# The context tile's expert selection done block by block, the weight ring's slots taken in turn, and norm rows combined ahead

## Chip, cores and metric

The kernel runs on one core of a Trainium2 chip. The metric is the time of one execution on the device in microseconds (us), as the median of several runs.

## What is computed

A transformer-like step of two layers over 128 context tokens and 512 latent tokens (width 1024, float32 throughout). In each layer the tokens pass a modulation, a combined input projection, a gated linear recurrence, grouped-query attention, a mix of the two branches and an output projection, a layer norm, and then a mixture of experts whose choice is the part that matters here:

```python
q = (x @ w_query).reshape(T, PEER_HEADS, 2, PEER_HALF)          # 8 heads, 2 halves of 128
s = jnp.einsum('thpd,hpnd->thpn', q, sub_keys)                  # 128 keys per half
s_top, i_top = lax.top_k(s, PEER_TOPK)                          # 16 of 128, per head and half
cand_s = s_top[:, :, 0, :, None] + s_top[:, :, 1, None, :]      # 16 x 16 sums per head
best_s, best_pos = lax.top_k(cand_s, PEER_TOPK)                 # 16 of 256
expert = jnp.take_along_axis(cand_i, best_pos, axis=-1)
gate = jax.nn.softmax(best_s, axis=-1)
# then, per token: gelu(x . u[expert]) * gate, summed over the rows v[expert]
x  = layer_norm(ALPHA * x + gate1 * (y @ w_out), ln1_g, ln1_b)
h2 = x * (1 + scale2) + shift2                                  # what the experts read
```

## The kernel before

The tokens lie in five tiles of 128: tile 0 is the context, tiles 1 to 4 are latent. All five engines run one instruction stream each, written out by hand, and are tied by semaphores. A loop of two passes runs over the layers.

**The weight ring.** Every dense weight comes in blocks of 2 MB into `ring`, which has two slots. SyncE's queue holds all loads of a layer in a fixed order (`load(s, block)`, L282 to L288): it waits until TensorE has released slot `s` (`w_free[s]`), then issues the transfer; TensorE waits on `w_full[s]`. A load that waits for its slot holds up all loads behind it. The 39 blocks of a layer are first taken in order, slot = block number mod 2; the last four of them (blocks 35 to 38) are the expert query weights, used for the context tile. Then blocks 25 to 38 (eight for the branch mix, two for the output projection, four for the queries) are loaded a second time, for the latent tiles, starting again with slot 0. After the fourth of these last query blocks comes the first block of the next layer, in slot 0.

**The context tile after attention.** TensorE makes the branch mix of the context tile (L1068), then the output projection in two halves (`tokenwise`, L722). VectorE adds the branch to `x` (`add_branch`, L1286 and L1288), takes the statistics of the layer norm (`norm_stats`, L1257 to L1261), gets a square root from ScalarE, and applies the norm in six steps (`norm_apply`, L1269 to L1279): subtract and scale, times gain, plus base (this is the new `x`), times scale2, plus shift2 (this is `h2c`). Only then TensorE turns `h2c` (L746), makes the four blocks of queries (`query_block`, L1096), each covering two heads, and behind each the scores of the block before (`score_block`, L1108). ScalarE copies queries (L615) and scores (L622) out of PSUM; after the fourth block of scores it signals `stage_ready` once. VectorE's `choose(gates[0])` then selects: 16 of 128 for 16 head halves (`first_level`, L1295 to L1306), the sums (`candidates`, L1512 and L1514), 16 of 256 for 8 heads (`second_level`), positions (L1525 to L1531), two look-ups of three steps over 2048 elements (L1537, L1541, L1544), and the expert numbers (L1548). With `stage_free` VectorE lets ScalarE write into `late` again, since `stage` and `work`, in which the selection works, are also the buffers `sg` of the latent mix. `idx_ready` lets GpSimd begin to gather the context tile's expert rows (L346).

**The latent mix.** TensorE goes on with eight blocks for the latent tiles (L1127), 32 matmuls of 512 columns each. Block n uses PSUM banks 0 to 3 when n is even and 4 to 7 when n is odd; the sigmoids of ScalarE (L641, behind `stage_free`) and the products of VectorE (`mix`, L1705, L1707) release them. VectorE puts 16 dot products of the context tile with gathered rows (L1660) behind each `mix`. Then follow the latent output projection (L722), the four norms of the latent tiles, the weighted sum of 96 gathered rows of the context tile on VectorE (`ctx_sum`, L1667) beside the latent queries and scores on TensorE (L1161, L1172), the last 32 of those rows on TensorE (L751, L753), the selection for the first latent tile (`choose(gates[1])`), and then the four latent tiles' experts, which take most of the kernel. The selections for the other latent tiles are cut in pieces between the dot products there (`piece`).

## Time and profile before

| | us |
|---|---|
| median of 3 runs | 6148.5 (6143.8 to 6161.4) |
| the profiled execution's own time | 6114.0 |
| its span, first to last instruction | 6112.2 |
| TensorE matmuls busy | 5046.7 (83%) |
| VectorE busy | 3742.0 (61%) |
| ScalarE busy | 825.7 (14%) |
| GpSimd busy | 1726.2 (28%) |

All times of the trace count from the start of the span. In a row of the timeline stand the start, the duration, the engine (PE is TensorE, DVE VectorE, ACT ScalarE, POOL GpSimd; SPq is SyncE's queue), the line of the kernel, the operation, what it writes and reads, and how many instructions are merged in the row; the number in brackets is how long the engine was idle before, with what ended it. A float32 matmul appears as two records. The first layer's stretch from the context norm to the first latent gathers is 1130 to 1720 us, the second layer's 4172 to 4760 us.

### The profile page before, as it was taken

What the parts mean: (1) busy time and instruction counts of PE and PEld (TensorE: products, weight loads), DVE (VectorE), ACT (ScalarE), POOL (GpSimd) and SP (SyncE); (2) the same over time, 40 slices, a digit from 0 to 9 for tenths busy, and PEclk for the clock granted to TensorE, in tenths of its full rate; (3) what the DMA queues carried; (4) which work ended last, traced back from release to release, by engine and by line L of the source; (5) the groups of instructions that cost most, each with busy time, mean ns of one, the idle gap of its engine ahead of it and who ended that gap; (6) DMA issues with size and microseconds to landing.
All of it is one profiled execution on the core that took longest, in us unless ns stands there. A gap on an engine that the chain in (4) does not pass through costs nothing. (4 is left out here: it accounts for less than half of the span.)

```text
span 6112.2 us, 62289 instructions
## 1 busy us (share of the span) xinstructions
PE 5046.7 (83%) x18696; PEld 2745.5 (45%) x18696; DVE 3742.0 (61%) x7541; ACT 825.7 (14%) x2126; POOL 1726.2 (28%) x1567
## 2 busy tenths in 40 slices
PE   5998789897977777777769987998979777777776
PEld 3787367643432222222237873676434322223222
DVE  0366333378888787876604663323788787878665
ACT  0121033000111001010101210330001110010100
POOL 0000000055644444443300000000657444444432
PEclk8999889998999999999989988899989899999999
DMA  6111100487999999999941111014979999999997
GB/s 230 45 47 46 46 1 27 180 331 296 385 373 400 409 403 411 398 416 421 368 179 45 46 46 46 1 43 177 346 295 379 374 407 409 403 412 396 416 421 328
DMA packets 251837, 1589.74 MB, mean 260 GB/s; under 512 B 28849, under 2 KB 38705, under 8 KB 105649
## 3 DMA queue, kind: packets, MB, share of 16 engines
q0 software_dynamic: 221184, 1342.28, 54.8%
q1 hardware_dynamic: 15936, 224.93, 9.6%
q10 hardware_dynamic: 14448, 19.42, 0.9%
q8 instruction: 112, 1.84, 0.1%
q14 instruction: 157, 1.28, 0.1%
HBM read 1581.27 MB, written 5.24 MB: 260 GB/s over the span
## 5 line engine op out<-in xcount | busy, mean ns | idle before, releaser
L751 PE MATMUL banks<-arena 128*128 128x512 f32 x1152 | 652.0, 649 | 304.4 <-PEq L1208 302.3
L365 POOL DMA_INDIRECT arena<-in_peer_uv,eidx x512 | 563.2, 1100 | 738.7 <-POOLq L364 708.8
L1646 DVE SCALAR_TENSOR_TENSOR arena<-arena 128x1024 f32<-128x1024 f32 x512 | 626.8, 1224 | 146.3 <-DMA arena<-in_peer_uv,eidx 133.7
L346 POOL DMA_INDIRECT arena<-in_peer_uv,eidx x512 | 592.5, 1157 | 335.9 <-POOLq L345 203.3
L753 PE MATMUL banks<-arena 128*128 128x512 f32 x1152 | 615.9, 617 | 0.0
L332 POOL COPY late<-arena 128x640 f32 x16 | 11.4, 719 | 1875.5 <-POOLq L331 1875.5
L417 ACT ACTIVATE late<-late 128x1 f32<-128x1 f32 (+1 forms) x1026 | 208.3, 203 | 2374.3 <-ACTq L416 2374.1
L751 PEld LDWEIGHTS banks<-arena 128*128 128x128 f32 x1152 | 202.0, 201 | 710.2 <-issue 709.8
L751 PE MATMUL banks<-ring,arena 128*128 128x512 f32 x512 | 301.1, 672 | 238.5 <-PEq L1208 238.5
L825 PE MATMUL banks<-hT,ring 128*128 128x320 f32 x1536 | 432.5, 433 | 2.9 <-PEq L822 2.9
L365 POOL DMA_INDIRECT ring<-in_peer_uv,eidx x256 | 286.3, 1118 | 477.3 <-POOLq L364 454.5
L753 PEld LDWEIGHTS banks<-arena 128*128 128x128 f32 x1152 | 230.1, 200 | 297.6 <-issue 297.6
L722 PE MATMUL banks<-ring,hT 128*128 128x512 f32 x800 | 349.1, 598 | 10.5 <-PEq L720 10.5
L1646 DVE SCALAR_TENSOR_TENSOR ring<-ring,arena 128x1024 f32<-128x1024 f32 x256 | 313.0, 1223 | 68.3 <-DMA ring<-in_peer_uv,eidx 67.6
L1646 DVE SCALAR_TENSOR_TENSOR hT<-hT,arena 128x1024 f32<-128x1024 f32 x256 | 313.7, 1225 | 61.4 <-DMA hT<-in_peer_uv,eidx 54.2
L365 POOL DMA_INDIRECT hT<-in_peer_uv,eidx x256 | 267.7, 1046 | 281.8 <-POOLq L364 264.0
L751 PE MATMUL banks<-hT,arena 128*128 128x512 f32 x512 | 284.6, 638 | 62.5 <-PEq L1208 60.1
L825 PEld LDWEIGHTS banks<-hT,ring 128*128 128x128 f32 x1536 | 283.9, 190 | 108.0 <-issue 4.5
L1660 DVE SCALAR_TENSOR_TENSOR arena<-arena,late 128x1024 f32<-128x1024 f32 x256 | 304.7, 1224 | 41.4 <-DMA arena<-in_peer_uv,eidx 33.6
L1638 DVE TENSOR_SCALAR arena<-ident,late,arena 128x128 f32<-128x128 f32 x512 | 210.3, 411 | 186.5 <-ACT late L417 169.8
L1638 DVE TENSOR_SCALAR arena<-ident,late 128x128 f32<-128x128 f32 x512 | 196.9, 385 | 178.7 <-ACT late L417 165.2
L753 PE MATMUL banks<-ring,arena 128*128 128x512 f32 x512 | 290.0, 651 | 0.0
(255 smaller groups left out, 7312.1 us busy)
## 6 DMA issues: line engine op xcount, KB each, us to landing
ring<-in_wblk SPq DMA_DIRECT2D x106, 2048.0 KB, 7.9
arena<-in_peer_uv,eidx POOLq DMA_INDIRECT x1024, 9.0
arena<-in_lnrows ACTq DMA_DIRECT2D x6, 1024.0 KB, 8.2
arena<-in_sk ACTq DMA_DIRECT2D x4, 1024.0 KB, 9.0
hT<-in_peer_uv,eidx POOLq DMA_INDIRECT x256, 11.9
ring<-in_peer_uv,eidx POOLq DMA_INDIRECT x256, 12.3
x<-in_x_sample ACTq DMA_DIRECT2D x1, 2048.0 KB, 18.3
late<-in_state ACTq DMA_DIRECT2D x32, 64.0 KB, 1.8
```

What stands on the lines that cost most here:

```text
L332: nc.gpsimd.tensor_copy(qstage[b], qkv[:, :, bass.ds((2 * i + b) * P, P)]).then_inc(qst_ready[b], 1)
L346: nc.gpsimd.indirect_dma_start(grow[j], None, ins["peer_uv"], bass.IndirectOffsetOnAxis(ap=eidx[:, n, r:r + 1].bitcast(U32), axis=0)).then ...
L365: nc.gpsimd.indirect_dma_start(gslot[j], None, ins["peer_uv"].rearrange("(e h) d -> e (h d)", h=2), bass.IndirectOffsetOnAxis(ap=eidx[:, n ...
L417: nc.scalar.activation(av[:, first:last], av[:, first:last], ACT.Gelu).then_inc(gelu_ready, 1)
L722: last = nc.tensor.matmul(banks[:, b, :], lhs[:, k, t * P:(t + 1) * P], ring[:, s, k, :], start=k == 0, stop=k == KD - 1)
L751: nc.tensor.matmul(banks[:, 4, :], diag[n], row[:, 0:CB], start=start, stop=stop, skip_group_check=True).then_inc(diag_used, 1)
L753: nc.tensor.matmul(banks[:, 5, :], diag[n], row[:, CB:D], start=start, stop=stop, skip_group_check=True).then_inc(free, 1)
L825: last = nc.tensor.matmul(banks[:, bank + f, 0:HALF], ring[:, b, k, c * P:(c + 1) * P], hT[:, k, tok], start=k == 0, stop=k == KD - 1)
L1638: V.tensor_scalar(diag[r % DIAGS], ident[:], av[:, r:r + 1], gate_of[:, r:r + 1], ALU.mult, ALU.mult).then_inc(diag_ready, 1)
L1646: V.scalar_tensor_tensor(u, u, 1.0, h2[:, t - 1, :], ALU.mult, ALU.mult, accum_out=av[:, r:r + 1])
L1660: V.scalar_tensor_tensor(grow[j], grow[j], 1.0, h2c, ALU.mult, ALU.mult, accum_out=av[:, r:r + 1]).then_inc(row_free[j], 1)
```

## The change

Three edits.

1. **Selection in blocks.** ScalarE signals `stage_ready` after each of the four score blocks. VectorE runs first level, sums, second level, positions and both look-ups for the two heads of a block as soon as its scores are there, four times; only the expert numbers are made once at the end. A new helper `look_up_both` does both look-ups of a block at once, one in `stage` and one in `work`. The exponential of the gates is still done once, after the last block.
2. **Ring slots in turn.** The second run of blocks 25 to 38 starts with slot 1 instead of slot 0, and TensorE's uses of them are swapped to match. The fourth latent query block so lies in slot 0, the third in slot 1.
3. **Norm rows combined ahead.** Before the context tile's branch is added, VectorE makes `scale = gain * (1 + scale2)` and `shift = shift2 + base * (1 + scale2)`. The statistics of each half are taken right behind that half's `add_branch`. After the first step of the norm, `h2c` is made straight from it in two steps and signalled; the new `x` is made after that.

```diff
@@ sync queue
                 load(0, l * NB + NB - 1)
-                with sp.Fori(0, (B_PQ - B_MIX) // 2) as i:
+                with sp.Fori(0, (NB - B_MIX) // 2) as i:
                     for s in range(2):
-                        load(s, l * NB + 2 * i + B_MIX + s)
-                with sp.Fori(0, (NB - B_PQ) // 2) as i:
-                    for s in range(2):
-                        load(s, l * NB + 2 * i + B_PQ + s)
+                        load(1 - s, l * NB + 2 * i + B_MIX + s)
@@ ScalarE, score_block
                     nc.scalar.copy(stage[:, n * CB:(n + 1) * CB], banks[:, b, :]).then_inc(bank_free[b], 1)
+                    act.drain().then_inc(stage_ready, 1)
...
                 score_block(3)
-                act.drain().then_inc(stage_ready, 1)
                 exponentiate(gates[0])
@@ TensorE
                 for n in range(KD):
-                    s, f = n % 2, n % 2
+                    s, f = (NB + n) % 2, n % 2
...
-                        tokenwise(2 * t - 2 + h, h, yT, t - 1).then_inc(to_dve[2 * t - 2 + h], 1)
+                        tokenwise(2 * t - 2 + h, 1 - h, yT, t - 1).then_inc(to_dve[2 * t - 2 + h], 1)
...
                 with pe.Fori(0, 2) as i:
-                    for s in range(2):
+                    for n in range(2):
+                        s = 1 - n
                         pe.wait_ge(w_full[s], 16)
...
@@ VectorE
+                def look_up_both(h):
+                    c, one = slice(h * TOPK, (h + 2) * TOPK), slice(h * TOPK * TOPK, (h + 2) * TOPK * TOPK)
+                    spots = [y[:, one] for y in (stage, work)]
+                    keys = tif[:, 2 * h:2 * h + 4].rearrange("p (h a) k -> p h a k", a=2)
+                    for a in range(2):
+                        V.tensor_tensor(r3(spots[a], TOPK), (paf, pbf)[a][:, c].unsqueeze(2).to_broadcast([P, 2 * TOPK, TOPK]),
+                                        iota[:].unsqueeze(1).to_broadcast([P, 2 * TOPK, TOPK]), ALU.is_equal)
+                    dve.drain()
+                    for a in range(2):
+                        spot = spots[a].rearrange("p (h s k) -> p h s k", h=2, s=TOPK)
+                        V.tensor_tensor(spot, spot, keys[:, :, a, :].unsqueeze(2).to_broadcast([P, 2, TOPK, TOPK]), ALU.mult)
+                    dve.drain()
+                    for a in range(2):
+                        V.tensor_reduce((e1, e2)[a][:, c], r3(spots[a], TOPK), AX.X, ALU.add)
                     dve.drain()
...
+                dve.wait_ge(ln_full, 16)
+                dve.sem_inc(ln_full, -16)
+                gain, base, scale, shift = ln1_ctx[:, 0], ln1_ctx[:, 1], bc_ctx[:, 1], bc_ctx[:, 2]
+                V.tensor_tensor(rows_ctx, base, scale, ALU.mult)
+                dve.drain()
+                V.tensor_tensor(shift, shift, rows_ctx, ALU.add)
+                V.tensor_tensor(scale, scale, gain, ALU.mult)
+                xc, stats, mv = x[:, 0, :], small[:, 64:76], small[:, 128:130]
                 for h in range(2):
                     add_branch(0, h, 4 + h, bc_ctx, tmp_ctx)
-                dve.wait_ge(ln_full, 16)
-                dve.sem_inc(ln_full, -16)
-                norm_stats(0)
-                norm_apply(0, ln1_ctx, bc_ctx, h2c)
-                choose(gates[0])
+                    V.bn_stats(stats[:, 6 * h:6 * h + 6], xc[:, h * CB:(h + 1) * CB])
+                dve.drain()
+                V.bn_aggr(mv, r3(stats, 6))
+                dve.drain()
+                V.tensor_scalar(small[:, 0:1], mv[:, 1:2], EPS, None, ALU.add)
+                inverse_root(1)
+                V.tensor_scalar(xc, xc, mv[:, 0:1], small[:, 0:1], ALU.subtract, ALU.mult)
+                dve.drain()
+                V.tensor_tensor(h2c, xc, scale, ALU.mult)
+                dve.drain()
+                V.tensor_tensor(h2c, h2c, shift, ALU.add).then_inc(h2_ready, 1)
+                V.tensor_tensor(xc, xc, gain, ALU.mult)
+                dve.drain()
+                V.tensor_tensor(xc, xc, base, ALU.add)
+                for n in range(4):
+                    dve.wait_ge(stage_ready, 1)
+                    dve.sem_inc(stage_ready, -1)
+                    first_level(stage, 4 * n, 4 * n + 4)
+                    candidates(2 * n, 2 * n + 2)
+                    second_level(2 * n, 2 * n + 2)
+                    positions(gates[0], 2 * n, 2 * n + 2)
+                    look_up_both(2 * n)
+                expert_ids()
```

`candidates` and `positions` get a range of heads; without it they do all eight, as before.

## Rows read from the trace of the kernel before

**Rows 1.** The page: its first line.
```profile
span 6112.2 us, 62289 instructions
```

**Rows 2.** Timeline of TensorE, first layer, queries and scores to latent mix.
```profile
1149.35 1.94 PE L746 MATMUL banks<-ident,late 128*128 128x128 f32 x8 [11.94 <-PEq L744]
1152.71 8.86 PE L1096 MATMUL banks<-hT,ring 128*128 128x128 f32 x64 [1.43 <-PEq L1093]
...
1171.11 7.38 PE L1096 MATMUL banks<-hT,ring 128*128 128x128 f32 x64 [0.20 <-PEq L1093]
...
1196.10 16.00 PE L1127 MATMUL banks<-hT,ring 128*128 128x512 f32 x32 [6.48 <-PEq L1125]
...
1254.35 13.97 PE L1127 MATMUL banks<-hT,ring 128*128 128x512 f32 x32 [0.41 <-PEq L1125]
```

**Rows 3.** The same timeline in the second layer.
```profile
4194.79 10.10 PE L1096 MATMUL banks<-hT,ring 128*128 128x128 f32 x64 [1.43 <-PEq L1093]
...
4239.18 16.80 PE L1127 MATMUL banks<-hT,ring 128*128 128x512 f32 x32 [5.77 <-PEq L1125]
```

**Rows 4.** Timeline of SyncE's queue and time to landing, window 1170 to 1200.
```profile
1187.55 0.93 SPq L286 DMA_DIRECT2D ring<-in_wblk  x2
...
DMA to landing us min/median/max: 8.3/10.4/12.5
```

**Rows 5.** Windows: span, then busy time by engine, PEclk, DMA share, GB/s.
```profile
1190.00:1196.00 6.00, 0.00 (x0) 0.00 (x0) 5.42 (x34) 0.32 (x1) 0.00 (x0) 0.78 1.00 425
1196.00:1200.00 4.00, 3.90 (x5) 1.85 (x6) 4.00 (x31) 0.00 (x0) 0.00 (x0) 0.50 0.78 332
```

**Rows 6.** Timeline of VectorE, first layer, the context norm.
```profile
1130.05 0.69 DVE L1286 TENSOR_TENSOR arena<-banks,arena 128x512 f32<-128x512 f32 x1 [9.45 <-DVEq L1285]
...
1139.22 1.29 DVE L1257 BATCH_NORM_STATS2 small<-x 128x6 f32<-128x512 f32 x2 [0.18 <-DVEq L1686]
...
1143.92 1.22 DVE L1273 TENSOR_TENSOR x<-x,arena 128x1024 f32<-128x1024 f32 x1
```

**Rows 7.** Timeline of ScalarE: first score copy and first latent sigmoids.
```profile
1171.03 0.58 ACT L622 COPY late<-banks 128x512 f32<-128x512 f32 x1 [0.95 <-ACTq L621]
...
1246.79 1.09 ACT L641 ACTIVATE late<-banks 128x512 f32<-128x512 f32 x2
```

**Rows 8.** Timeline of VectorE, first layer, the context selection.
```profile
1227.84 0.29 DVE L1525 TENSOR_TENSOR late<-late 128x128 f32<-128x128 f32 x1
...
1228.91 2.29 DVE L1537 TENSOR_TENSOR late<-late,iota 128x2048 f32<-128x2048 f32 x1
...
1243.10 0.29 DVE L1548 SCALAR_TENSOR_TENSOR late<-late 128x128 f32<-128x128 f32 x1
...
1249.54 0.69 DVE L1707 TENSOR_TENSOR arena<-late 128x512 f32<-128x512 f32 x1
```

**Rows 9.** Timeline of VectorE: the selection's first instruction and its wait.
```profile
1190.50 2.61 DVE L1295 MAX8 late<-late 128x8 f32<-128x128 f32 x13 [41.45 <-DVEq L1567]
```

**Rows 10.** Timeline of TensorE and VectorE, first layer, latent output projection and third norm.
```profile
1434.69 57.36 PE L722 MATMUL banks<-ring,arena 128*128 128x512 f32 x128 [6.20 <-PEq L720]
...
1495.42 0.16 DVE L1269 RECIPROCAL small<-small 128x1 f32<-128x1 f32 x1 [4.36 <-DVEq L1268]
```

**Rows 11.** Groups by line, VectorE, windows 1519 to 1664 and 4563 to 4704.
```profile
L1667 DVE SCALAR_TENSOR_TENSOR late<-arena,late 128x1024 f32<-128x1024 f32 x96 | 123.3, 1285 | 20.7 <-DMA arena<-in_peer_uv,eidx 11.2 <-issue 2.4
...
L1667 DVE SCALAR_TENSOR_TENSOR late<-arena,late 128x1024 f32<-128x1024 f32 x96 | 123.3, 1284 | 16.3 <-DMA arena<-in_peer_uv,eidx 6.7 <-issue 2.4
```

**Rows 12.** Timelines of SyncE's queue, VectorE and TensorE in and behind the weighted sum.
```profile
1621.90 0.33 SPq L286 DMA_DIRECT2D ring<-in_wblk  x1
...
1632.21 8.17 DVE L1667 SCALAR_TENSOR_TENSOR late<-arena,late 128x1024 f32<-128x1024 f32 x6 [2.68 <-DMA arena<-in_peer_uv,eidx]
...
1663.45 3.19 DVE L1295 MAX8 late<-late 128x8 f32<-128x128 f32 x16 [0.29 <-DVEq L1567]
...
1652.70 1.15 PE L1172 MATMUL banks<-arena 128*128 x8 [0.31 <-PEq L1170]
```

More of the change, by code:

```diff
@@ L182, in build @@
         tmp_ctx = arena[:, 20480:20992]
+        rows_ctx = arena[:, 20992:22016]
         tmp_lat = arena[:, 5120:5632]
@@ L1183, in _ @@
                             if u:
-                                score_part(8 * i + 4 * s + u - 1, u - 1)
-                        score_part(8 * i + 4 * s + 3, 3)
+                                score_part(8 * i + 4 * n + u - 1, u - 1)
+                        score_part(8 * i + 4 * n + 3, 3)
                         pe.drain().then_inc(w_free[s], 1)
@@ L1509, in first_level, with candidates @@
                           work[:, a * NKEYS:b * NKEYS], NKEYS, b - a)
-                def candidates():
-                    V.tensor_copy(tif, ti.bitcast(U32))
-                    halves_v = tv.rearrange("p (h a) k -> p h a k", a=2)
-                    V.tensor_tensor(stage.rearrange("p (h a b) -> p h a b", h=PEER_H, a=TOPK),
-                                    halves_v[:, :, 0, :].unsqueeze(3).to_broadcast([P, PEER_H, TOPK, TOPK]),
-                                    halves_v[:, :, 1, :].unsqueeze(2).to_broadcast([P, PEER_H, TOPK, TOPK]), ALU.add)
+                def candidates(a=0, b=PEER_H):
+                    out = slice(a * TOPK * TOPK, b * TOPK * TOPK)
+                    V.tensor_copy(tif[:, 2 * a:2 * b], ti[:, 2 * a:2 * b].bitcast(U32))
+                    halves_v = tv[:, 2 * a:2 * b].rearrange("p (h a) k -> p h a k", a=2)
+                    V.tensor_tensor(stage[:, out].rearrange("p (h a b) -> p h a b", h=b - a, a=TOPK),
+                                    halves_v[:, :, 0, :].unsqueeze(3).to_broadcast([P, b - a, TOPK, TOPK]),
+                                    halves_v[:, :, 1, :].unsqueeze(2).to_broadcast([P, b - a, TOPK, TOPK]), ALU.add)
                     dve.drain()
@@ L1522, in second_level, with positions @@
                           work[:, a * n:b * n], n, b - a)
-                def positions(gate_of):
-                    V.tensor_tensor(r3(gate_of, TOPK), r3(bs, TOPK), r3(bs, TOPK)[:, :, 0:1]
-                                    .to_broadcast([P, PEER_H, TOPK]), ALU.subtract).then_inc(soft_ready, 1)
-                    V.tensor_scalar(bq.bitcast(U32), bp.bitcast(U32), 4, None, ALU.logical_shift_right)
-                    V.tensor_scalar(bp.bitcast(U32), bp.bitcast(U32), 15, None, ALU.bitwise_and)
-                    dve.drain()
-                    V.tensor_copy(paf, bq.bitcast(U32))
-                    V.tensor_copy(pbf, bp.bitcast(U32))
+                def positions(gate_of, a=0, b=PEER_H):
+                    c = slice(a * TOPK, b * TOPK)
+                    high, low4 = bq[:, c], bp[:, c]
+                    op = V.tensor_tensor(r3(gate_of[:, c], TOPK), r3(bs[:, c], TOPK), r3(bs[:, c], TOPK)[:, :, 0:1]
+                                         .to_broadcast([P, b - a, TOPK]), ALU.subtract)
+                    if b == PEER_H:
+                        op.then_inc(soft_ready, 1)
+                    V.tensor_scalar(high.bitcast(U32), low4.bitcast(U32), 4, None, ALU.logical_shift_right)
+                    V.tensor_scalar(low4.bitcast(U32), low4.bitcast(U32), 15, None, ALU.bitwise_and)
+                    dve.drain()
+                    V.tensor_copy(paf[:, c], high.bitcast(U32))
+                    V.tensor_copy(pbf[:, c], low4.bitcast(U32))
+                    dve.drain()
@@ L1682, in _ @@
                 dve.sem_inc(bc_ready, -1)
+                dve.wait_ge(ln_full, 16)
[6 more added lines that the diff above has]
+                xc, stats, mv = x[:, 0, :], small[:, 64:76], small[:, 128:130]
                 for h in range(2):
                     add_branch(0, h, 4 + h, bc_ctx, tmp_ctx)
-                dve.wait_ge(ln_full, 16)
-                dve.sem_inc(ln_full, -16)
-                norm_stats(0)
-                norm_apply(0, ln1_ctx, bc_ctx, h2c)
-                choose(gates[0])
+                    V.bn_stats(stats[:, 6 * h:6 * h + 6], xc[:, h * CB:(h + 1) * CB])
[10 more added lines that the diff above has]
+                V.tensor_tensor(xc, xc, gain, ALU.mult)
+                dve.drain()
+                V.tensor_tensor(xc, xc, base, ALU.add)
[8 more added lines that the diff above has]
+                expert_ids()
                 V.tensor_scalar(e1, e1, layer_base[:], 2.0, ALU.add, ALU.mult)
```

## The prediction

> **What bounds the kernel now.** I read the page first [rows 1]: the span is 6112.2 us, the profiled execution's own time 6114.0, so 1.8 us lie around the span. The median of the runs shown is 6148.5, 34 us more than the profiled one; nothing in the trace tells why, so I work out a difference inside the profiled span and subtract it from the median. The change touches a stretch of some 100 us in each layer, so shares of the whole say nothing. I followed the chain of each layer from the context norm to the first latent gathers in the timelines.
>
> In the stretch TensorE is the engine that sets the pace, with two holes. It idles 11.94 us before it turns `h2c` [rows 2], because VectorE's norm chain runs meanwhile [rows 6]. And it idles 6.48 us (5.77 in the second layer) before the latent mix [rows 2, 3]. What ends the second hole is a weight load: SyncE issues two loads together at 1187.55 [rows 4], right after the last query block of the context has left slot 0 (L1096; four blocks, the last ends about 1187.2), and the first lands 8.3 us later, at 1195.9; the mix starts at 1196.10. The second of the two loads went into slot 1, free some 8.7 us earlier; it had only stood behind the first in the queue. In that hole the DMA share is 1.00 and TensorE's granted clock falls: 0.78 over the hole, 0.50 over the next 4 us, its lower level of 1.2 GHz [rows 5]. So the first half block of the mix takes 16.00 and 16.80 us where the later ones take 13.97 [rows 2, 3].
>
> VectorE's selection starts at 1190.50 after 41.45 us without work [rows 9] and ends its last look-up at 1243.10 [rows 8]. It looks like the bottleneck, but is not: what waits for it is PSUM bank 0, which ScalarE's first sigmoid behind `stage_free` releases at 1246.79 + 0.6 = 1247.4 [rows 7], and TensorE wants it for the third mix block at 1254.35 and gets it with an idle time of only 0.41 us [rows 2]. There are 7.0 us of slack.
>
> **Part 1, norm rows ahead.** Added before the norm: three instructions over 1024 elements, 1.22 us each and 0.08 between them [rows 6], 3.9 us together. VectorE idles 9.45 us just there [rows 6], waiting for the output projection, so they cost nothing; without that cover they would cost 3.9. The gain rows they read were loaded at the start of the stage, long before. Removed from the chain to `h2_ready`: one half of the statistics (half of 1.29), now taken in the idle time before the second half arrives, about 0.65; two full-width steps, 2 x 1.30 = 2.6; the wait before the statistics that shows 0.18 [rows 6], of which I count 0.05. Sum 3.3 us per layer. The two steps for the new `x` come behind, 2.6 us, while VectorE has nothing to do until the first scores. Everything on TensorE after it moves 3.3 us earlier. The hole is then 8.6 us. The clock also fell within a hole of 6.5 us [rows 5], so it will be low again: the first query block takes 8.86 or 10.10 us against 7.38 [rows 2, 3], a price of 1.5 to 2.7 us that I leave as it is; its bounds are a gain of 1.2 and a loss of 1.2 per layer.
>
> **Part 2, ring slots in turn.** The first mix load no longer needs slot 0 but slot 1, left by the third query block, which ends at 1171.11 + 7.38 = 1178.5 [rows 2]. Issue at 1178.8, landing 8.3 later [rows 4], 1187.1. TensorE finishes the last scores at 1196.10 - 6.48 = 1189.6. So the load is there 2.5 us before it is wanted, and all of this shifts together by part 1. The hole goes down to the 0.41 us that stands between blocks: 6.07 us in the first layer, 5.36 in the second. With no hole the clock does not fall, and the slow start goes as well: 16.00 - 13.97 = 2.03 and 16.80 - 13.97 = 2.83. Sum 8.1 and 8.2 us. Which wait is late next? The third mix block. It moves from 1254.35 to 1254.35 - 3.3 - 8.1 = 1242.95, and the bank it needs would come at 1247.4 - 3.3 = 1244.1 with the old selection, a stall of 1.1 us. That is all that part 3 is worth on the path. The later blocks of the mix take 28 us each and need one load each, so they are unaffected. In the wait before the latent output projection, 6.20 us [rows 10], a load follows the last mix block in both orders: nothing changes there. The two issues that follow in SyncE's queue after the first mix load go at the same releases as before, or earlier.
>
> The Trainium skill ("TensorE: Matmul & The Clock Gate", The HAM clock gate) says that where the clock changes depends on when the chip happens to look, so that the same kernel has a different number of slow matmuls from run to run. The two layers here agree (2.03 and 2.83). By that page the 4.9 us that I count for the clock in the two layers could be anything between 4 and 6 in a given run.
>
> One more effect lies 450 us later. In the weighted sum the VectorE waits for gathered rows because weight loads share the DMA engines. In the first layer these waits sum to 11.2 us and in the second to 6.7 [rows 11]. The first layer has one load more: the next layer's first block, issued at 1621.90 when the third latent query block has left slot 0; 7.6 us later VectorE falls dry for 2.68 us [rows 12]. In the changed order slot 0 holds the fourth query block, whose last scores end at 1652.70 + 1.15 = 1653.9 [rows 12], so that load is issued at 1654.1 - 11.4 = 1642.7. The weighted sum ends at about 1663.2 [rows 12] - 11.4, and without the stall at 1647.4, that is 4.7 us after the issue and before the 7.6 us have passed. So 11.2 - 6.7 = 4.5 us go, once. Bounds: 0, if the load now delays the 32 rows that TensorE sums after it, and 4.5. TensorE takes 1.72 us for a row and has eight of them gathered ahead, 13.8 us, against one load of 8 to 12 us [rows 4]. I take 4.4.
>
> **Part 3, selection in blocks.** Work: before, 1243.10 - 1190.50 = 52.6 us [rows 8, 9]. Look-ups were 14.2 (1228.91 to 1243.10) as six instructions of 2.29; now per block six of 512 elements, in pairs, 0.69 each [rows 8] with 0.08 behind each pair's end, about 4.15, times four 16.6. Three more calls each of first and second level, 0.5 us each for waiting out their five steps (an estimate from gaps of 0.1 us between steps), 3.0. Sums and positions in four small sets instead of one, about 3.7 more. Together 61.8 us. Lower bound 52.6 (nothing added); upper bound 67, if each of the 39 added small instructions cost 0.29, as 128 elements do [rows 8], and the calls 3.0. It starts when the first score block is copied, 1171.03 + 0.58 [rows 7] - 3.3 = 1168.3. Blocks of scores come every 8.7 us, a block of selection takes 15.4, so VectorE never waits again and ends at 1230.1, with bounds 1221 and 1235. From the last look-up to bank 0 it took 4.3 us, so the bank is free at 1234.4, 8.5 us before the 1242.95 at which it is wanted. The drain and the signal that ScalarE adds behind each score copy hold up only its next query copy, which it waits 7 us for anyway. GpSimd starts its gathers 13 us earlier, but VectorE's first dot products still stand behind the second mix block, so this gains nothing.
>
> The Trainium skill ("VectorE: DVE Perf Modes", The TRN2 errata) speaks against this part: every VectorE instruction has a fixed cost whatever its size. This trace agrees, 0.69 us for 512 elements where a quarter of 2.29 is 0.57 [rows 8]; by the page's 58 cycles the 18 added look-up instructions would cost 1.1 us (an estimate), half of my 2.4.
>
> **Does it reach the end?** The latent output projection follows the mix directly (57.36 us [rows 10]); the square root of the third latent norm waits for TensorE's turn behind it, 4.36 us [rows 10], so VectorE hangs on TensorE there, and from then on the fourth norm, the weighted sum and the second selection on VectorE. All of it moves with the mix. The gathers of the latent tiles start behind that selection.
>
> Sum: first layer 3.3 + 8.1 + 4.4 = 15.8; second layer 3.3 + 8.2 = 11.5; together 27.3 us. The profiled execution would take 6086.7, the median 6148.5 - 27.3 = **6121.2 us**.
>
> **Rivals.**
> - *The load only moves its stall.* The next layer's first block delays the rows that TensorE adds, and the 4.4 come back: gain 22.9, 6125.6. For it: TensorE's sum of 32 rows gates the fourth latent gather. Chance 0.15.
> - *The hole stays.* The mix load, though issued earlier, lands late, because it collides with the load of the fourth query block, or the slot is released later than I read. Then only part 1 and the 4.4 are left, 6.6 + 4.4 = 11 us: 6137.5. Against it: two loads together took 8.3 and 12.5 us [rows 4], and they are issued over 8 us apart now. Chance 0.1.
> - *The expert stages swallow it.* They fill the rest of both layers and hang on gathers; a shift may change how transfers meet, and the gain is within 18 us: about 6138. Chance 0.1.
> - *Slower: the selection becomes the bound.* VectorE's small instructions cost much more than their rows, and the third mix block waits for `stage_free`. It begins to show at 61.8 + 8.5 = 70.3 us of selection, and the layer is slower than before from 70.3 + 11.4 = 82, that is 20.4 us a block. At 25 us a block the selection takes 100 and each layer loses 18: 6148.5 + 36 - 4.4 = 6180. Against it: no row has an instruction at such a price. Chance 0.04.
>
> **How the numbers follow.** The forecast has 0.61. Its own uncertainties (clock 2.4, runs of the same kernel that differ by up to 18 us around the median) give 6110 to 6132. The range takes in the first three rivals: 6108 to 6139. About 0.3%, 18.4 us, is what a measurement can tell from no change. Faster by more than that: nearly all of the forecast and of the first rival, 0.75. Within: the second and third and what run-to-run spread takes, 0.21. Slower: 0.04.
>
> **What the profile will show.** TensorE's idle time before the first L1127 is near 0.4 us and its first row 13.97; the granted clock stays at 1.00 there. Idle before L746 is about 8.6. VectorE's first MAX8 comes 22 us earlier, and its last look-up 13 us. No wait for the bank in the third mix block. The load for the next layer falls behind the weighted sum, whose DMA waits drop to about 7. The prediction is wrong if TensorE still waits before the mix, if the selection takes over 70 us, or if the stretch is 11 us shorter and the span is not.

## The result, and the profile after

| | median us | range | runs |
|---|---|---|---|
| before, same measurement | 6153.0 | 6143.8 to 6162.6 | 6 |
| after | 6122.7 | 6117.3 to 6133.6 | 6 |

The ratio is 0.995 with a 95% interval of 0.9936 to 0.9964: 30.4 us less, with an interval of 22 to 39 us, clear of no change. The forecast was 27.3 us less. The profiled execution of the changed kernel took 6133.6 us, 11 us over its median, whereas that of before was 34 us under the median of its own runs. So the two traces must not be subtracted as wholes: the spans are 6112.2 and 6131.8, as if the kernel had become slower. What follows compares stretches.

The page of the changed kernel, its first line and the line of busy times; VectorE has 84 instructions and 21 us more than before:

```profile
span 6131.8 us, 62461 instructions
...
PE 5046.9 (82%) x18696; PEld 2744.1 (45%) x18696; DVE 3763.4 (61%) x7625; ACT 825.4 (13%) x2126; POOL 1722.6 (28%) x1567
```

Timeline of TensorE, changed kernel, first layer, from the turn of `h2c` (L744, before L746) over the last scores (L1106) and the latent mix (L1125) to the latent output projection (L720). The last line is from a later window of the same view:

```profile
1148.24 1.94 PE L744 MATMUL banks<-ident,late 128*128 128x128 f32 x8 [8.63 <-PEq L742]
...
1186.25 2.02 PE L1106 MATMUL banks<-arena 128*128 128x128 f32 x16 [0.41 <-PEq L1104]
1188.11 13.90 PE L1125 MATMUL banks<-hT,ring 128*128 128x512 f32 x32
...
1244.27 13.97 PE L1125 MATMUL banks<-hT,ring 128*128 128x512 f32 x32 [0.41 <-issue]
...
1427.00 57.07 PE L720 MATMUL banks<-ring,arena 128*128 128x512 f32 x128 [8.56 <-PEq L1136]
```

Against [rows 2]: the idle time before the turn is 8.63 instead of 11.94, there is no idle time at all before the mix where 6.48 stood, the first half block takes 13.90 instead of 16.00, and the third mix block begins without a wait (0.41). Of the four, the first three are the gain. The last line has 8.56 against 6.20 in [rows 10], for a wait that I had put at no change; more traces below say whether that is a loss.

The same view in the second layer:

```profile
4200.23 1.94 PE L744 MATMUL banks<-ident,late 128*128 128x128 f32 x8 [8.63 <-PEq L742]
...
4241.74 13.90 PE L1125 MATMUL banks<-hT,ring 128*128 128x512 f32 x32
...
4478.61 57.03 PE L720 MATMUL banks<-ring,arena 128*128 128x512 f32 x128 [6.23 <-PEq L718]
```

Windows of the changed kernel over the end of the scores and the start of the mix (span, then busy time of TensorE's matmuls and weight loads, VectorE, ScalarE, GpSimd, then the granted clock, the DMA share and GB/s). Where the clock was 0.78 and 0.50 and the DMA share 1.00 [rows 5], it is now 1.00 throughout, and the transfers are spread out:

```profile
1184.00:1190.00 6.00, 5.59 (x38) 4.47 (x37) 5.59 (x27) 1.76 (x3) 0.00 (x0) 1.00 0.53 167
1190.00:1200.00 10.00, 10.00 (x24) 4.39 (x24) 8.88 (x37) 0.00 (x0) 0.00 (x0) 1.00 0.29 121
```

Timeline of VectorE, changed kernel, context selection: the first row opens the first block of two heads, the next is one of its three look-up rows, and the two MAX8 rows open the second and the third block; the last row is the step that makes the expert numbers:

```profile
1170.48 0.87 DVE L1294 MAX8 late<-late 128x8 f32<-128x128 f32 x4 [20.10 <-DVEq L1731]
...
1182.04 1.29 DVE L1545 TENSOR_TENSOR late<-late,iota 128x512 f32<-128x512 f32 x2
...
1186.24 0.87 DVE L1294 MAX8 late<-late 128x8 f32<-128x128 f32 x4 [0.18 <-DVEq L1731]
...
1202.20 0.87 DVE L1294 MAX8 late<-late 128x8 f32<-128x128 f32 x4 [0.18 <-DVEq L1731]
...
1233.24 0.29 DVE L1570 SCALAR_TENSOR_TENSOR late<-late 128x128 f32<-128x128 f32 x1
```

A block takes 15.8 and 16.0 us (forecast 15.4), the whole from 1170.48 to 1233.5 63.1 us (forecast 61.8, upper bound 67). ScalarE's first sigmoid of the mix follows, timeline of ScalarE:

```profile
1236.92 1.08 ACT L639 ACTIVATE late<-banks 128x512 f32<-128x512 f32 x2
```

so the bank that the third mix block needs is free at about 1237.5, 6.8 us before 1244.27, where TensorE takes it.

**How much of the gain stands behind the mix?** I measure from the start of the idle time before the turn (start of that row minus its bracket, which is where the context's output projection ends) to the start of the latent output projection.

| | layer 1 | layer 2 | both |
|---|---|---|---|
| before | 1434.69 - 1137.41 = 297.3 | 4479.13 - 4179.48 = 299.7 | |
| after | 1427.00 - 1139.61 = 287.4 | 4478.61 - 4191.60 = 287.0 | |
| less | 9.9 | 12.6 | 22.5 |
| forecast | 11.4 | 11.5 | 22.9 |

**The weighted sum, where the last 4.4 us were to come from.** Groups of VectorE by line, changed kernel, weighted sum in the first layer, against [rows 11]. The waits for gathered rows did fall, from 11.2 to 5.9 us, as forecast (6.7):

```profile
L1689 DVE SCALAR_TENSOR_TENSOR late<-arena,late 128x1024 f32<-128x1024 f32 x96 | 123.3, 1284 | 15.4 <-DMA arena<-in_peer_uv,eidx 5.9 <-issue 2.1
```

But look at what comes behind the sum, timeline of VectorE:

```profile
1647.10 2.66 DVE L1689 SCALAR_TENSOR_TENSOR late<-arena,late 128x1024 f32<-128x1024 f32 x2 [0.26 <-DMA arena<-in_peer_uv,eidx]
1681.01 3.19 DVE L1294 MAX8 late<-late 128x8 f32<-128x128 f32 x16 [31.24 <-DVEq L1589]
```

The latent selection starts 31 us after the sum has ended, where in [rows 12] it followed at once (0.29). What it waits for are the latent scores, which come late because TensorE has holes among the latent queries. Timeline of TensorE, changed kernel, and of ScalarE, which copies those scores:

```profile
1554.11 2.07 PE L1170 MATMUL banks<-arena 128*128 x8 [7.13 <-issue]
1574.45 15.54 PE L1159 MATMUL banks<-hT,ring 128*128 128x512 f32 x32 [18.27 <-issue]
```

```profile
1561.89 0.27 ACT L669 COPY late<-banks 128x128 f32 x1 [8.28 <-ACTq L668]
...
1573.56 0.27 ACT L669 COPY late<-banks 128x128 f32 x1 [11.02 <-ACTq L668]
```

The "issue" in brackets means that the profile shows nothing for which TensorE waited. The ends of matmuls in a row are modelled; ScalarE's copies say when scores really were there. The last group of scores of the first query block, which by the first row ended at 1556.2, was copied at 1573.56, the group before it at 1561.89. TensorE was not waiting for weights: SyncE's queue, below, shows that the slot that TensorE leaves with these scores was free only at 1574.76, and that signal is TensorE's own. Then the windows of the same 10 us, first the changed kernel, then the kernel before:

```profile
1574.76 1.40 SPq L287 DMA_DIRECT2D ring<-in_wblk  x1
```

```profile
1555.00:1565.00 10.00, 1.18 (x6) 0.88 (x5) 9.27 (x8) 0.65 (x2) 7.59 (x8) 0.50 0.97 365
```

```profile
1555.00:1565.00 10.00, 9.25 (x29) 4.66 (x28) 9.27 (x8) 1.98 (x5) 7.84 (x8) 1.00 1.03 396
```

Both kernels gather expert rows at full DMA share there. In the one TensorE is busy for 1.18 us of 10, in the other for 9.25. Either the change made these holes, or the profiled execution of before happened to be without them. That was the first question for the runs.

### The profile page after: what moved, and what is told of

It reads as the page before. It is cut to its first block and busy times, and to the rows that moved or that the text cites. A ratio compares the mean times of both kernels' runs of the same rounds, so it can differ in the third digit from the quotient of the medians.

```text
span 6131.8 us, 62461 instructions
## 1 busy us (share of the span) xinstructions
PE 5046.9 (82%) x18696; PEld 2744.1 (45%) x18696; DVE 3763.4 (61%) x7625; ACT 825.4 (13%) x2126; POOL 1722.6 (28%) x1567
## 3 DMA queue, kind: packets, MB, share of 16 engines
q14 instruction: 158, 1.29, 0.1%
## 5 line engine op out<-in xcount | busy, mean ns | idle before, releaser
L330 POOL COPY late<-arena 128x640 f32 x16 | 11.4, 720 | 1873.2 <-POOLq L329 1873.2
L720 PE MATMUL banks<-ring,hT 128*128 128x512 f32 x800 | 350.6, 600 | 10.6 <-PEq L718 10.6
```

The source lines that it names most:

```text
L330: nc.gpsimd.tensor_copy(qstage[b], qkv[:, :, bass.ds((2 * i + b) * P, P)]).then_inc(qst_ready[b], 1)
L720: last = nc.tensor.matmul(banks[:, b, :], lhs[:, k, t * P:(t + 1) * P], ring[:, s, k, :], start=k == 0, stop=k == KD - 1)
```

## Experiments

Each group below ran on one chip, with runs of the kernel before between its own. Ratios are against those. The quoted texts are what was expected of each kernel before it ran.

### Are the holes the change's, and what is each part worth?

`before_again` and `after_again` are the two kernels unchanged. `ring_only` has only the ring's edits, `norm_only` only those of the norm rows:

```diff
# ring_only, against the kernel before
-                        load(s, l * NB + 2 * i + B_MIX + s)
+                        load(1 - s, l * NB + 2 * i + B_MIX + s)
...
-                    s, f = n % 2, n % 2
+                    s, f = (NB + n) % 2, n % 2
# norm_only, against the kernel before
-                norm_stats(0)
-                norm_apply(0, ln1_ctx, bc_ctx, h2c)
+                V.tensor_tensor(scale, scale, gain, ALU.mult)
...
+                V.tensor_tensor(h2c, xc, scale, ALU.mult)
```

Expected of `before_again`:

> The kernel before, unchanged, profiled a second time. In the profile of the changed kernel TensorE has holes among the latent queries (L1159: 18.3 and 5.3 us in the first layer, 11.3 and 4.5 in the second, 7.1 before a score in each), which the first profile of the kernel before had nowhere. Theory H, the holes come from the state of the chip and visit both kernels: they show here too, in L1161 and L1172, and this profiled execution is near the timed runs (about 6150) and not at 6114. Theory C, they belong to the change: none here, and the profiled execution is again near 6114. Ratio of the times 1.000 by both.

Expected of `after_again`:

> The changed kernel, unchanged, profiled a second time and timed again. By the sum of the prediction the time is 27.3 us under that of the kernel before, ratio 0.9956. Theory C: the holes in the latent queries are at the same places with the same lengths. Theory H: they are of other lengths or elsewhere, and the span minus the holes is about 6085.

Expected of `ring_only`:

> The kernel before with the ring slots in turn and nothing else. By the prediction's terms: the hole before the latent mix goes (6.1 and 5.4 us, with 2.0 and 2.8 us of slow clock), but the third mix block then waits about 1.1 us for bank 0, and the weighted sum of the first layer loses 4.4 us of DMA waits: 18.5 us in all, ratio 0.9970. The rival that the hole stays because the load lands late gives 4.4 us, ratio 0.9993. If the holes in the latent queries belong to the swapped slots (theory C) they show here.

Expected of `norm_only`:

> The kernel before with the norm rows combined ahead and nothing else. By the prediction: TensorE's idle time before it turns h2c falls from 11.94 to about 8.6 us, 3.3 us in each layer, 6.6 in all, ratio 0.9989; the hole before the latent mix stays at 6.5 and 5.8 us. If the price of the slow clock behind the shorter hole were lower, up to 1.2 us more in each layer. The rival that the norm chain is hidden gives 1.000.

| | median us | ratio | 95% interval |
|---|---|---|---|
| kernel before, 35 runs | 6202.9 | | |
| before_again | 6203.4 | 0.9997 | 0.9985 to 1.0009 |
| after_again | 6186.1 | 0.9974 | 0.996 to 0.9989 |
| ring_only | 6195.7 | 0.9988 | 0.9974 to 1.0001 |
| norm_only | 6208.8 | 1.0008 | 0.9997 to 1.002 |

Everything is some 50 us slower on this chip, the kernel before included, and the change is worth 17 us here, with an interval of 7 to 25. The waits say why the level is higher. TensorE and VectorE in `before_again` (engine, what it writes, line, what ended the wait; then us in total, times, longest), first layer, latent queries and selection:

```profile
PE banks L1161 <- issue: 23.3, 1, 23.3
PE banks L1172 <- ACTq L665: 17.3, 1, 17.3
...
PE banks L1172 <- issue: 11.9, 1, 11.9
```

```profile
DVE late L1295 <- DVEq L1567: 52.1, 1, 52.1
```

and the same two views of `after_again`:

```profile
PE banks L1159 <- issue: 33.1, 1, 33.1
PE banks L1170 <- issue: 16.1, 2, 15.8
```

```profile
DVE late L1294 <- DVEq L1589: 50.7, 1, 50.7
```

The kernel before has the holes too, and its selection waits 52 us for the scores. So the change does not make them: theory C falls, and they visit both kernels, as theory H has it. The first profile of before was the one profiled execution, of all ten with these gathers, that had none. It also says where that execution was fast. From the start of the latent output projection to the copy of the first latent tile's expert numbers on GpSimd (L354, in the changed kernel L352) it took 282.4 and 277.9 us in the two layers. The profiled execution of the changed kernel, on the same chip, took 307.7 and 298.7, 46 us more; it had gained 22.5 before that point, and its span is 19.6 us longer. So the missing holes account for that execution's lead over the changed kernel's. That they are also the 34 us between it and the median of its own runs, which the prediction left open, is likely, but no run without a profile shows its holes.

The medians cannot tell the single parts apart beside these holes: `norm_only` should have gained 6.6 and lost 5.9, `ring_only` should have gained 18.5 and gained 7.2, with intervals 14 to 17 us wide. The traces can in part. The stretch of the table above, both layers together, is 599.0 us in `before_again`, 573.7 in `after_again` (25.3 less) and 591.8 in `ring_only` (7.2 less). TensorE's third mix block in `ring_only`, first and second layer, shows one reason why the ring alone is worth less, a wait where the kernel before has 0.41:

```profile
1251.31 15.67 PE L1124 MATMUL banks<-hT,ring 128*128 128x512 f32 x32 [2.33 <-PEq L1122]
...
4331.89 13.97 PE L1124 MATMUL banks<-hT,ring 128*128 128x512 f32 x32 [2.32 <-PEq L1122]
```

To compare times, the holes had to go.

### The same four kernels without the holes

Gathers are the heaviest traffic in that stretch (27.65 of 31.44 MB between 1540 and 1620 us in the first profile of the changed kernel). These four kernels leave out the context tile's second gather, that of the `v` rows, and let the weighted sum read whatever the buffers hold from the first; the arithmetic of every engine stays, and each wait for a row stays with the count of the gathers that are left. TensorE's 32 rows are changed in the same way (not shown).

```diff
                         pool.sem_inc(row_free[j], -1)
+                        if n:
+                            continue
                         nc.gpsimd.indirect_dma_start(
...
-                        dve.wait_ge(row_full[j], ((l * 2 + 1) * TURNS + r // ROWS + 1) * 16)
+                        dve.wait_ge(row_full[j], (l * TURNS + TURNS) * 16)
```

`nov_before` and `nov_after` are the two kernels with this edit, `nov_norm` has only the norm rows of the change, `nov_ring_norm` has norm rows and ring but the old selection of eight heads at once.

Expected of `nov_before`:

> The kernel before without the gathers of the context tile's 128 v rows in each layer (the weighted sum is taken over rows that already lie there, so the output of the context experts is left out); the transfers beside the latent queries so go down to the weight loads. Theory D, the holes of 15 to 42 us that TensorE has among the latent queries come from the gathers that fill the DMA engines there: none are left, and the time falls by their two lengths and the DMA waits of the weighted sum, some 60 to 90 us on a chip where the kernel before takes 6203. Theory E, they come from TensorE's own instructions or its clock: they stay, and the time falls by under 20 us.

Expected of `nov_after`:

> The changed kernel with the same gathers left out. Without them the weighted sum has no DMA waits, so the 4.4 us that the prediction books there can't appear, and by its other terms the time is 11.4 + 11.5 = 22.9 us under nov_before's, a ratio 0.0037 lower. If theory D holds this pair measures the change without the holes: 22 to 24 us. If the change were worth no more than the 17 us of after_again for other reasons, it is 17 here too.

Expected of `nov_ring_norm`:

> As nov_after, but with the context selection as it was (after all four score blocks). By the prediction the third mix block then waits about 1.1 us for bank 0 in each layer: 2.2 us over nov_after. The view that VectorE's long selection is what bounds this stretch gives 13 us in each layer over nov_after, 26 in all, so no gain at all over nov_before.

Expected of `nov_norm`:

> The kernel before with the norm rows combined ahead alone, and the v gathers left out. By the prediction 6.6 us under nov_before (3.3 in each layer). If a shorter hole also made the clock come back at another moment, up to 1.2 us in each layer either way.

| | median us | ratio to the kernel before | 95% interval | less than nov_before |
|---|---|---|---|---|
| kernel before, 9 runs | 6212.1 | | | |
| nov_before | 6095.7 | 0.981 | 0.9797 to 0.9824 | |
| nov_norm | 6090.2 | 0.9804 | 0.979 to 0.9817 | 5.5 |
| nov_ring_norm | 6081.8 | 0.9796 | 0.9783 to 0.981 | 14.0 |
| nov_after | 6074.0 | 0.9776 | 0.9761 to 0.979 | 21.7 |

Without those gathers the kernel before is 116 us faster, 1.9%, more than the 60 to 90 expected. It is all in one stretch: from the latent output projection to the expert numbers it takes 273.1 and 272.9 us in the two layers of `nov_before`, 329.9 in each of `before_again` (on another chip). The holes are gone: waits of TensorE over the same stretch, `nov_before`, whose largest entry at the latent queries (L1163) is four waits of 0.4 to 1.5 us, and VectorE's wait before the selection, `nov_before` and then `nov_after`:

```profile
PE banks L1163 <- PEq L1161: 3.3, 4, 1.5
```

```profile
DVE late L1297 <- DVEq L1569: 3.4, 1, 3.4
```

```profile
DVE late L1296 <- DVEq L1591: 2.1, 1, 2.1
```

So theory D holds: the gathers' transfers and the holes belong together, and theory E, by which the holes come without them, falls. What in the gathers slows TensorE is not shown.

The change is worth 21.7 us here; the ranges of the two kernels' five runs do not touch. By the same stretches as above: from the norm's idle time to the latent output projection 297.8 against 286.1 us in the first layer, 298.7 against 288.3 in the second, 22.1 together. TensorE's rows of `nov_before`, first layer (turn, first mix block):

```profile
1142.01 1.94 PE L748 MATMUL banks<-ident,late 128*128 128x128 f32 x8 [11.94 <-PEq L746]
...
1188.24 16.09 PE L1129 MATMUL banks<-hT,ring 128*128 128x512 f32 x32 [6.46 <-PEq L1127]
```

of `nov_norm`, where the first gap has shrunk by 3.3 us and the second stays, as does the slow start:

```profile
1145.02 1.94 PE L749 MATMUL banks<-ident,late 128*128 128x128 f32 x8 [8.64 <-PEq L747]
...
1192.94 16.68 PE L1130 MATMUL banks<-hT,ring 128*128 128x512 f32 x32 [6.62 <-PEq L1128]
```

and of `nov_ring_norm` (first and third mix block of the first layer, third and fourth of the second):

```profile
1180.12 13.90 PE L1127 MATMUL banks<-hT,ring 128*128 128x512 f32 x32
...
1238.57 15.67 PE L1127 MATMUL banks<-hT,ring 128*128 128x512 f32 x32 [2.70 <-PEq L1125]
```

```profile
4255.85 15.67 PE L1127 MATMUL banks<-hT,ring 128*128 128x512 f32 x32 [2.71 <-PEq L1125]
...
4289.00 11.40 PE L1127 MATMUL banks<-hT,ring 128*128 128x512 f32 x26 [3.75 <-PEq L1125]
```

The hole before the mix is gone, and the old selection, which now ends too late, makes a new one before the third block: 2.70 instead of 0.41, and behind it 15.67 instead of 13.97, 4.0 us in each layer and 8.0 in both. `nov_after` beats this kernel by 7.7 us in the medians, though the ranges of their runs overlap, and by 9.5 in the stretches (583.8 against 574.4). In `nov_after` the third block starts after 0.41 again. So selecting in blocks is worth more than the 1.1 us a layer that I gave it.

The 3.75 us before the fourth block of the second layer (3.54 at the same place in `ring_only`) are something else. Timeline of VectorE in `nov_ring_norm`, its product with the last bank of the third block:

```profile
4288.71 0.69 DVE L1724 TENSOR_TENSOR late<-late,banks 128x512 f32<-128x512 f32 x1 [4.23 <-DVEq L1723]
```

By TensorE's rows the matmuls into that bank ended at 4285.3. VectorE had waited for them since 4284.5 and began at 4288.71. So TensorE finished late there too, beside the first gather, that of the `u` rows, which these kernels keep (DMA share 1.03 from 4285 to 4289). Why it does so with the old selection and not with the new is not shown.

### Are the instruction transfers to blame for the holes?

The latent queries run in a loop of two passes, and instruction transfers of 16 KB lie in that stretch. `after_third` is the changed kernel unchanged; `queries_unrolled` writes TensorE's loop out:

```diff
-                with pe.Fori(0, 2) as i:
+                for i in range(2):
                     for n in range(2):
```

Expected of `after_third`:

> The changed kernel once more, as the base for the two kernels below that carry the change further. Ratio to the kernel before between 0.995 and 0.9975, as in the two earlier measurements.

Expected of `queries_unrolled`:

> The changed kernel with TensorE's loop over the latent queries written out, two passes instead of a loop of two; same work, more instructions to bring in while the gathers run (TensorE's instruction transfers of 16 KB came twice in the first pass and not at all in the second). Theory F, the holes come where TensorE's instructions are brought in late under full DMA engines: there are holes in the second pass too, and the time is 20 to 80 us over the changed kernel's. Theory G, the instruction transfers have nothing to do with it: same time within 0.15%, holes at the old places.

The two took 6119.7 (0.9946, 0.9932 to 0.996) and 6120.7 us (0.9953, 0.994 to 0.9967), on a chip where the kernel before takes 6150.5. TensorE's second, third and fourth query block in the first layer, `after_third` and then `queries_unrolled`:

```profile
1560.55 16.93 PE L1159 MATMUL banks<-hT,ring 128*128 128x512 f32 x32 [10.60 <-issue]
...
1603.35 16.02 PE L1159 MATMUL banks<-hT,ring 128*128 128x512 f32 x32 [7.98 <-PEq L1157]
...
1637.65 13.97 PE L1159 MATMUL banks<-hT,ring 128*128 128x512 f32 x32 [0.41 <-PEq L1179]
```

```profile
1550.47 16.73 PE L1159 MATMUL banks<-hT,ring 128*128 128x512 f32 x32 [8.90 <-issue]
...
1591.29 16.80 PE L1159 MATMUL banks<-hT,ring 128*128 128x512 f32 x32 [6.40 <-issue]
...
1626.18 13.97 PE L1159 MATMUL banks<-hT,ring 128*128 128x512 f32 x32 [0.41 <-PEq L1157]
```

The holes stand at the same two places, whether the loop branches or not, and the time is the same. In the second layer `after_third` has one more, 5.58 us before the fourth block, where `queries_unrolled` has 0.41. Theory F, as put down, falls. The transfers themselves speak against it too. The page counts 112 transfers of 16 KB in every kernel and 116 in `queries_unrolled`, the only one with more instructions for TensorE alone, so they are TensorE's. In the first layer's latent queries they lie at 1515 and 1578 us in `after_third` and at 1511, 1569 and 1618 in `queries_unrolled`: while TensorE works, in none of the holes, and none ends one.

### Can the wait for the scores be used?

VectorE waits 18 to 66 us before the latent selection in the profiles with holes. `blocks_96` selects for the first latent tile in four blocks as well, each as soon as its scores are there; `blocks_104` also takes eight more of the weighted sum's rows onto VectorE.

```diff
-CTX_ROWS = 96
+CTX_ROWS = 104
...
-                act.drain().then_inc(stage_ready, 1)
+                        act.drain().then_inc(stage_ready, 1)
...
-                choose(gates[1])
+                choose_blocks(gates[1])
```

Expected of `blocks_96`:

> The changed kernel with the first latent tile's selection in blocks of two heads as well, so that three of the four blocks are done before TensorE's late last scores. VectorE then is done some 35 us earlier where TensorE is late, but the 32 rows that TensorE adds after the queries take 55 us and free the buffers of the first latent gathers: they become the bound, so 0 to 10 us less than the changed kernel. In an execution without holes it would be 8 us a layer longer on VectorE.

Expected of `blocks_104`:

> As blocks_96, and VectorE adds 104 rows instead of 96, TensorE 24 instead of 32. TensorE ends 13.8 us earlier, VectorE has 11 us more that fall into time it now waits. 20 to 35 us less than the changed kernel where TensorE's holes are 20 us and more a layer; 10 to 20 us more than it where there are none.

They took 6118.2 (0.9947, 0.9933 to 0.996) and 6118.9 us (0.9951, 0.9937 to 0.9964), against 6119.7: no difference, which the first expectation allows. The second, 20 to 35 us less, missed, although the holes of `after_third` were 26 and 21 us in the two layers. VectorE's waits around the first selection, `after_third` (first fence) and `blocks_96`:

```profile
DVE late L1294 <- DVEq L1589: 24.8, 1, 24.8
...
DVE small L1578 <- DVEq L1577: 3.4, 1, 3.4
```

```profile
DVE small L1578 <- DVEq L1577: 14.5, 1, 14.5
...
DVE late L1294 <- DVEq L1602: 0.8, 4, 0.3
```

The wait before the first MAX8 went from 24.8 to 0.8 us. But the blocks cost some 10 us more of VectorE than the selection at once (63.1 in the changed kernel's context tile against 52.6), and 11.1 us more are waited behind it, for the exponential of the gates (L1578). The first latent gather starts at 1721.1 instead of 1725.5 us in the first layer and at 4769.8 instead of 4764.5 in the second (the context norm 3.5 us later in the first, at the same time in the second). Neither version beats the changed kernel.

## Why the prediction came out as it did

The total was near: 30.4 us measured where 27.3 were forecast, inside the range. By its steps:

- **Norm rows ahead, 3.3 us a layer.** Exact: 11.94 to 8.63 in both layers, and 8.63 to 8.72 in every kernel that has the edit. The added instructions before the norm cost nothing: VectorE still has 5.5 us without work there (9.45 before, less the 3.9 forecast). `nov_norm` gained 5.5 us where 6.6 were forecast, within what the medians can tell.
- **The hole before the mix, 6.1 and 5.4.** It went in both layers of every kernel with the new slots, and the 0.41 us that I left standing went as well. The rival in which the hole stays is out.
- **The slow start, 2.0 and 2.8.** The first half block takes 13.90 in both layers. The Trainium skill ("TensorE: Matmul & The Clock Gate", The HAM clock gate) has it that the point at which the clock changes depends on when the chip happens to look. The traces agree: in the five kernels that keep this hole (`before`, `before_again`, `norm_only`, `nov_before`, `nov_norm`) the slow start costs 2.0 to 3.0 us a layer and 4.4 to 5.4 in both, where I had 4.9 and expected 4 to 6.
- **The wait before the latent output projection, put at no change.** It is the landing of a load, and it varies. In the changed kernel's trace it cost 2.4 us in the first layer (8.56 against 6.20) and gave back 0.5 in the second (6.23 against 6.69), which is why the first layer gained 9.9 instead of 11.4 and the second 12.6. Over all traces it is no step of the change: with the old slots it is 4.1 to 8.3 us, mean 6.5 in ten layers, with the new ones 3.7 to 9.1, mean 6.8 in eighteen. So no change was right, and the 9.9 is chance. The mean of the whole stretch is 298.7 us over three traces of the kernel before (`before`, `before_again`, `nov_before`) and 286.8 over four of the changed one (`after`, `after_again`, `after_third`, `nov_after`): 23.9 us in both layers where 22.9 were forecast.
- **Next layer's load behind the weighted sum, 4.4 once.** The mechanism was there: the waits for rows fell to 5.9 (forecast 6.7). But this step failed: the 4.4 us are off the path in every profiled execution with these gathers but the first, since the selection behind the sum, where it is done at once, waits 18 to 66 us for TensorE's scores. I had read from [rows 12] that the sum's end sets the start of the selection (idle 0.29). That row came from the one execution in which it does. In effect the first rival's sum, 22.9, is what the traces support, though not for the rival's reason, a delay of TensorE's rows; `nov_after` measured 21.7.
- **Where the other 7.5 us of the 30.4 come from** is not shown, and they need no cause: 22.9 lies at the edge of the interval (22 to 39). The same pair of kernels gave 30.4, 30.8 and, on the chip with the larger holes, 17 us; the mean of the three, 26, is 3 over the sum of the terms. That the forecast of 27.3 came nearer to 30.4 than 22.9 would have is luck, since it holds 4.4 us that were not there.
- **Selection in blocks.** Its length was forecast at 61.8 and is 63.1, its end 6.8 us before it is needed instead of 8.5. What I mis-sized is what its absence would cost: I put the bank at 1.1 us late. It was 2.3 late (2.70 against 0.41), and the slow clock that I priced for the other hole and not for this one came to 1.7 more. In the sum this changed nothing, because the change has the selection in blocks. A reader who had costed the parts alone would have left this one out.
- **The expert stages** did not swallow the gain, and the slower rival had no basis: no instruction of the selection cost more than its row. The look-up rows are 1.29 us for two instructions of 512 elements, as [rows 8] have it for one (0.69 each, less what overlaps). By these rows (0.69 us for 512 elements, 2.29 for 2048) an instruction has a fixed part of 0.16 us, so that the 58 cycles from which the prediction got 1.1 us for 18 added instructions are too few; it would be 2.8 for instructions one by one (an estimate from the two rows).

## What to carry to other kernels

When a queue takes its loads strictly in order, let each load ask for the slot that is released first; a load that could have started 8 us earlier was only standing behind another. When a hole is closed upstream, ask at once who becomes late behind it, and price that wait with the slow clock that it can bring. And before a stall is counted as gain, look at more than one execution: the row that said it was on the path came from the only one where it was.

## What was unexpected of the hardware

- **A TensorE that is late without a wait.** Among gathers at a DMA share of 0.95 to 1.01, TensorE finishes its last scores of a block 17 us after the row says in the first trace of the changed kernel and 22 us in `before_again` (1575.6 by the row, copied at 1598.01). The granted clock is 0.77 and then 0.50 while it does next to nothing (1.18 us of 10). Leaving out the gathers of the context tile's `v` rows in both layers makes the kernel 116 us faster. TensorE's 16 KB instruction transfers lie outside the holes, and unrolling the loop changed nothing. Whether it is the weights that reach the array late or something else that the gathers crowd out stays open. A full DMA share alone is not enough: the first profile of before had it too (1.01 from 1540 to 1650 us) and TensorE was busy 107 of those 110 us.
- **A short hole can be enough for the clock, and need not be.** 2.3 to 2.7 us without work before the third mix block made it 1.7 us longer (15.67 against 13.97) in three of the four layers of `ring_only` and `nov_ring_norm`, and not in the fourth (2.32 us, then 13.97). The 3.5 to 3.8 us by the rows before the fourth block cost nothing behind them. 5.8 to 6.6 us before the first mix block cost 2.0 to 3.0 in all ten layers that have them.
- **The same kernel is up to 1% apart on different chips** (6150 to 6212 us for the kernel before), and one execution can be 34 us under the median of its own runs.
